# The high halves of a mixer's weight tiles: from GpSimd to ScalarE

## The reference

```python
h = rmsnorm(x, norm_pre_mix) * (1 + scale_m) + shift_m      # scale, shift, gate: silu(c) @ w_ada + b_ada
proj = h @ w_in                                             # the widest product of the block
# attention: 12 heads of 128 in three dilated groups, rotary, softmax, sum over groups
y_attn  = attention(proj[...]) @ w_attn_out
# 16 DeltaNet heads: short convolution, silu, l2norm, gated delta rule in chunks, rmsnorm, silu gate
y_delta = gated_delta_rule(proj[...]) @ w_delta_out
y = (sigmoid(gates_a) * y_attn + sigmoid(gates_d) * y_delta) @ w_mix_out
x = x + gate_m * rmsnorm(y, norm_post_mix)
# then a PEER feed-forward block: queries, top-16 of 128 x 128 experts, gelu, weighted sum of expert rows
```

## Time and profile before

| | |
|---|---|
| Median of 3 executions | 5580.42 us (5576.69 to 5580.77) |
| Profiled execution, its own time | 5584.36 us |
| Its span, first to last instruction | 5582.6 us |
| Mean granted TensorE clock | 0.970 |
| TensorE busy | 5186.8 us (93%) |
| VectorE busy | 2819.2 us (51%) |
| ScalarE busy | 1427.8 us (26%) |
| GpSimd busy | 2954.6 us (53%) |

### The profile page before, as it was taken

How to read it: one execution, slowest core, us unless ns; L and a number is a source line. 1 busy time by engine, 2 the same in 40 slices (tenths; PEclk the granted TensorE clock), 3 DMA queues, 4 the chain that set the end, 5 groups by cost and what they waited for, 6 DMA issues and landing times.

```text
span 5582.6 us, 67218 instructions
## 1 busy us (share of the span) xinstructions
PE 5186.8 (93%) x25699; PEld 4417.7 (79%) x25699; DVE 2819.2 (51%) x4370; ACT 1427.8 (26%) x2021; POOL 2954.6 (53%) x1124
## 2 busy tenths in 40 slices
PE   3877899998999899999989999999999999999997
PEld 1666778777777777877858888888888799999997
DVE  7777730455555545224367756664000056666764
ACT  2100010133232332100032233333222233333332
POOL 1454457644444444577734443334444478888883
PEclk6988899999999999999999999999999999999999
DMA  7444422311111111232323334344333479988994
GB/s 303 177 166 177 175 97 90 121 61 60 56 60 60 61 56 62 73 120 105 112 105 110 111 126 148 133 149 151 132 121 119 138 247 317 316 314 308 317 316 146
DMA packets 245042, 839.93 MB, mean 150 GB/s; under 512 B 24080, under 2 KB 89744, under 8 KB 200624
## 3 DMA queue, kind: packets, MB, share of 16 engines
q1 hardware_dynamic: 127632, 562.09, 29.0%
q10 hardware_dynamic: 94752, 141.98, 7.5%
q0 software_dynamic: 22528, 134.30, 6.3%
HBM read 766.91 MB, written 71.37 MB: 150 GB/s over the span
## 4 chain that ended last, share of the span: by engine, by line
PE 71%; DVE 13%; issue 7%; DMA 4%; ACT 2%; POOL 1%; ACTq 1%; SPq 0%; DVEq 0%
PE bank L835 9%; PE bank L837 9%; PE bank L839 9%; PE bank L518 7%; PE bank L520 6%; PE bank L522 6%; PE bank L932 5%; PE bank L934 5%; PE bank L933 5%; DVE hacc L1555 4%; DMA half<-ada_late 3%; PE bank L898 2%; PE wide L743 1%; PE wide L732 1%; DMA raw<-stream 1%
## 5 line engine op out<-in xcount | busy, mean ns | idle before, releaser
L460 POOL TENSOR_TENSOR lo<-raw,hi 128x1024 fp32r<-128x1024 f32 x528 | 1279.0, 2424 | 1147.1 <-ACT hi L1244 1143.5
L444 POOL TENSOR_TENSOR hi<-raw,ones 128x2048 fp32r<-128x2048 f32 x168 | 610.6, 3635 | 1354.8 <-PE bank L522 1084.7
L518 PE MATMUL bank<-xh,hi 128*128 128x512 f32 x2624 | 1111.9, 424 | 39.1 <-DVE xl L1485 11.5
L520 PE MATMUL bank<-xl,hi 128*128 128x512 f32 x2624 | 1040.0, 396 | 0.0
L522 PE MATMUL bank<-xh,lo 128*128 128x512 f32 x2624 | 1039.5, 396 | 0.0
L835 PE MATMUL bank<-xh,hi 128*128 128x512 f32 x2176 | 858.9, 395 | 8.8 <-DVE xl L1485 8.8
L1244 ACT ACTIVATE hi<-raw 128x1024 fp32r<-128x1024 f32 x528 | 546.7, 1056 | 1215.4 <-PE bank L839 1043.4
L837 PE MATMUL bank<-xl,hi 128*128 128x512 f32 x2176 | 848.0, 390 | 0.0
L839 PE MATMUL bank<-xh,lo 128*128 128x512 f32 x2176 | 847.7, 390 | 0.0
L447 POOL TENSOR_TENSOR lo<-raw,hi 128x2048 fp32r<-128x2048 f32 x168 | 819.2, 4876 | 13.2
L932 PE MATMUL bank<-CH,hi 128*128 128x384 f32 x2048 | 694.5, 339 | 16.1 <-DVE R L1944 8.3
(11 more groups left out here) (275 smaller groups left out, 5985.7 us busy)
## 6 DMA issues: line engine op xcount, KB each, us to landing
raw<-stream SPq DMA_DIRECT2D x528, 512.0 KB, 3.9
raw<-stream SPq DMA_DIRECT2D x184, 1024.0 KB, 4.8
half<-ada_late SPq DMA_DIRECT2D x128, 512.0 KB, 3.9
act_d<-etile ACTq DMA_DIRECT2D x128, 256.0 KB, 2.0
G_d<-stage ACTq DMA_DIRECT2D x12, 2048.0 KB, 7.5
Gt<-G_d ACTq DMA_DIRECT2D x32, 768.0 KB, 15.3
cf<-act_d ACTq DMA_DIRECT2D x31, 768.0 KB, 18.1
arow<-stream SPq DMA_DIRECT2D x16, 1024.0 KB, 7.3
```

What stands on the lines that cost most here:

```text
L444: nc.gpsimd.tensor_tensor(hi[slot][:, :], raw[s][:, :], ones[:, 0:1].to_broadcast([P, D]), ALU.mult).then_inc(hi_done, 1)
L460: nc.gpsimd.tensor_tensor(lo_h[slot], raw_h[h % 4], hi_h[slot].bitcast(F32), ALU.subtract).then_inc(f_lo[h % 4], 1)
L518: nc.tensor.matmul(out, hi[slot][:, w], at_k(xh, k), start=(k == 0), stop=False, skip_group_check=True)
L520: nc.tensor.matmul(out, hi[slot][:, w], at_k(xl, k), start=False, stop=False, skip_group_check=True)
```

## The change

`split` goes. GpSimd waits only for `hi_done` and subtracts. ScalarE gets `high(s, turn)`, a copy of the whole tile that waits for the raw tile and for the slot's unit, at written-out places in its own order: the two first tiles in steps 6 and 10 of the making of `h`; behind the copy of each attention unit and each gate unit; in a loop of their own for `w_attn_out` and `w_delta_out`; in the DeltaNet ahead of the unit's tanh, behind `ahead_of_unit`; for `w_mix_out` ahead of the square of each row block.

```diff
         @block.gpsimd
         def _(pool):
-            def split(s, slot, landed, free, count):
-
-                pool.wait_ge(raw_full[s], landed)
-                if free is not None:
-                    pool.wait_ge(unit_done[slot], free + ONE)
-                nc.gpsimd.tensor_tensor(hi[slot][:, :], raw[s][:, :], ones[:, 0:1].to_broadcast([P, D]), ALU.mult
-                                        ).then_inc(hi_done, 1)
-                pool.wait_ge(hi_done, count)
-                nc.gpsimd.tensor_tensor(lo[slot][:, :], raw[s][:, :], hi[slot][:, :].bitcast(F32),
-                                        ALU.subtract).then_inc(raw_used[s], 1)
-
-            pool.wait_ge(s_const, 1)
-            for s in (2, 3):
-                pool.wait_ge(arow_used[s], ADA_USES + ONE)
             with pool.Fori(0, MIX_USES) as i:
                 for s in range(2):
-                    split(s, s, (ADA_USES + 1 + i) * 16, i, i * 2 + s + 1)
+                    pool.wait_ge(hi_done, i * 2 + s + 1)
+                    nc.gpsimd.tensor_tensor(lo[s][:, :], raw[s][:, :], hi[s][:, :].bitcast(F32), ALU.subtract
+                                            ).then_inc(raw_used[s], 1)
...
+            def high(s, turn):
+
+                act.wait_ge(raw_full[s], (turn + (ADA_USES + 1)) * 16)
+                act.wait_ge(unit_done[s], turn + ONE)
+                nc.scalar.activation(hi[s][:, :], raw[s][:, :], ACT.Copy).then_inc(hi_done, 1)
+
...
                     shifted(k - 1, R1, R1, part(SHIFT_M), s_hr)
+                if k in (6, 10):
+                    s = (k - 6) // 4
+                    act.wait_ge(arow_used[2 + s], ADA_USES + ONE)
+                    high(s, 0)
...
                     nc.scalar.activation(dst[:, :], bank[u % 2][:, :], ACT.Copy).then_inc(bank_free[u % 2], 1)
+                    high(u % 2, u // 2 + 1)
...
+                high(s, i + (B_GA // 2 + 1))
...
+            for w in range(U_WAO):
+                high(w % 2, (B_WAO + w) // 2 + 1)
             act.wait_ge(s_waoc, 3 * U_WAO)
...
                     if not first:
                         ahead_of_unit(h - 1, j)
+                    high(j % 2, h * 2 + (B_DN // 2 + j // 2 + 1))
                     if j < 3:
                         act.wait_ge(d_e, h * 3 + j)
...
+                high(s, i + (B_GD // 2 + 1))
...
+            for u in range(U_WDO):
+                high(u % 2, (B_WDO + u) // 2 + 1)
             act.wait_ge(unit_done[1], B_MIX // 2 + ONE)
...
             for k in range(KT):
+                if k < U_MIX - 2:
+                    high(k % 2, (B_MIX + k) // 2 + 1)
                 act.wait_ge(bank_free[k % 2], B_MIX // 2 + k // 2 + 1)
```

## The result

| | before | after |
|---|---|---|
| median | 5580.6 us (5576.69 to 5588.56, 4 runs) | 5481.31 us (5479.76 to 5484.19, 4 runs) |
| ratio | | 0.9821 [0.9804, 0.9838] |
| profiled execution, and its span | 5584.36, 5582.6 us | 5480.44, 5478.6 us |

The kernel is 99 us faster (104 in the profiled executions).

What follows compares the result with a forecast made beforehand. VectorE, held up by GpSimd and with the DMA loop of `half`, was taken to pace attention. Terms: -51 attention, +5 start, +4.4 DeltaNet, -3 product starts, +1 last attention-out tile = -43.6 us; forecast 5537 us, range 5500 to 5580.

Steps and rivals of the forecast that it cites:

- the attention term: Attention stretch: VectorE is held up less by GpSimd and units get shorter, 1.5 us a unit, -51 us.
- 75 us is the most if all returns: Attention: upper bound of the gain, 36 high halves with about 2.1 us of VectorE waiting in each.
- the start: First tiles: ScalarE's high half comes late, TensorE starts 7 us later, first product near 134; taken as +5 us.
- The replay: Attention: one cycle of two units, 38.1 us from softmax to softmax, worked through; 3.6 us shorter.
- The price that the prediction feared: Attention: a VectorE operation in flight makes GpSimd's low half wait; at worst 28 us off the 51, leaving 23.
- The DeltaNet: DeltaNet heads: low halves end later in three of four units, earlier in the fourth; +0.3 us a head, +4.4 us.
- The step that I replayed first: DeltaNet, behind the unit ending at 1571.6: `q` becomes free, but `bt` and TensorE's next step end 0.54 us later.
- Gate units: Gate stretch: the split takes 7.3 us after a unit's end, covered by TensorE's next unit of 10.5; unchanged.
- delta-out and mix-out products: Their starts wait for the same lock, which ends 1 to 1.5 us earlier each: -3 us with both.
- The low half's end is all that counts: Rival, chance 0.12: VectorE's work is caught by the low half anyway; attention gives only 20 us, 5567 us.
- ScalarE's order makes the DeltaNet slower: Rival, chance 0.14: high halves ahead of each convolution's tanh delay TensorE, 5.8 us a head; 38 us slower, 5618.
- The DeltaNet gains too: Rival, chance 0.10: the shorter lock removes a third of the DeltaNet's 105 us idle, 35 us more; 5497 us.

Runs made afterwards that it cites:

- relock: Kernel after, with GpSimd's old multiplication put back ahead of the low halves of tiles 2 to 37, ScalarE still making the high halves: 5581.73 us.
- nolock: Kernel after, with two GpSimd fills, which read nothing, and two one-column operations ahead of the low halves of tiles 2 to 37: 5499.36 us.
- experiment 4: Kernel after, with ScalarE making the first two high halves ahead of h instead of in its steps 6 and 10: 5477.13 us.
- light_hacc: Kernel before, with hacc, all but the first of each sum, on 128 of its 1024 columns: 5508.39 us against 5580.38.
- attention_only: Kernel after, but GpSimd splits as before for all but the first 38 tiles: 5488.21 us against 5582.03 for the kernel before.
- before_in_two: Kernel before, with both of GpSimd's halves in two pieces and nothing on ScalarE: 5532.14 us, ratio 0.9907 to before.
- rest_only: Kernel after, but GpSimd splits the first 38 tiles as before: 5573.22 us, ratio 0.9981 to before.
- low_two: Kernel after, with each low half as two GpSimd operations instead of one: 5403.07 us, ratio 0.9682 to before.
- early_low_four: Kernel after, with each low half in four pieces and ScalarE's first two high halves ahead of h: 5337.01 us, ratio 0.9552 to before.

## Why the prediction was wrong, point by point

**The step that failed is the attention term.** It was sized at -51 us, 1.5 a unit, with "75 us is the most if all returns". From TensorE's first product to the end of tile 36's low half the kernel took 777.8 - 127.2 = 650.6 us and now takes 669.7 - 132.7 = 536.9: -114, 3.2 for each of 35 units. With the start, -46 was forecast and -108 measured. The mechanism was the right one (relock and nolock), the size was off by a factor of two. Two places in the working can be pointed to, and a third, the clock, may have its part.

*The bound counted too little.* The 75 us were the waiting inside the high halves alone. But 33 of VectorE's 111 us come from the rotation of `qk`, which the low half had caught (4.43 us instead of 0.67 at 392.75) and which now runs ahead of it. When one hold goes, what stands behind it moves, and may escape the next one. The bound is then the whole waiting in the stretch, not the share of the instruction removed: the earlier trace rows had it, 154 us for `hacc` alone.

*The replay kept the old phase.* It moved each end by its own saving, but left TensorE's unit where it stood against VectorE's softmax. The timelines of VectorE and of GpSimd in the kernel after, one cycle of two units, for the earlier trace rows:

```profile
352.23 0.41 DVE L1537 SCALAR_TENSOR_TENSOR prob<-wide,acst 128x256 f32<-128x256 f32 x1
...
356.53 0.75 DVE L1550 TENSOR_SCALAR prob<-prob,mcol 128x1024 f32<-128x1024 f32 x1
...
357.80 0.67 DVE L1527 TENSOR_TENSOR qk<-qk,acst 32x512 f32<-32x512 f32 x1
...
359.11 2.67 DVE L1563 SCALAR_TENSOR_TENSOR hacc<-half,cond,hacc 128x1024 f32<-128x1024 f32 x2
363.71 4.98 DVE L1563 SCALAR_TENSOR_TENSOR hacc<-half,cond,hacc 128x1024 f32<-128x1024 f32 x2 [1.94 <-DMA half<-ada_late]
...
382.16 0.41 DVE L1537 SCALAR_TENSOR_TENSOR prob<-wide,acst 128x256 f32<-128x256 f32 x1
```

```profile
345.19 4.57 POOL L442 TENSOR_TENSOR lo<-raw,hi 128x2048 fp32r<-128x2048 f32 x1 [7.86 <-ACT hi L977]
360.86 5.36 POOL L442 TENSOR_TENSOR lo<-raw,hi 128x2048 fp32r<-128x2048 f32 x1 [11.09 <-ACT hi L977]
```

The cycle is 382.16 - 352.23 = 29.9 us; 38.1 was the old one and 34.6 the replay's. The low half begins 8.6 us behind the softmax's first step, in the replay 6.4. The rotation is done ahead of it in both. But in these 2.2 us two `hacc` get in as well (2.67 us for both, so free), which the replay had end with the low half. So the shorter cycle for VectorE changed what the low half meets. The price that the prediction feared shows in the same place: the low half takes 5.36 us because the second of them is still running. This account is read from two timelines; no run moves the phase alone.

**The granted clock.** In the attention stretch it is 0.98 after and 0.88 before, means over the levels of 2.4 and 1.2 GHz, and a multiplication takes 463.52/2097 = 0.221 us instead of 486.62/2046 = 0.238. What TensorE did before was to wait: the 64 us at L621 are gone. relock brings 0.89 back with the old waits, nolock has 0.96. Of the 114 us from the first product to tile 36, TensorE's busy time makes up 37 (547.3 to 510.5 us) and its idle time 77 (103.4 to 26.5). So the clock moves with the hold. How much of the gain is its own can't be told apart, since no run changes it alone: in a stretch that VectorE paces, TensorE's shorter busy time need not shorten anything. The prediction held TensorE's own 487 us fixed.

**The start**, +5 for the start with a first product near 134: it is at 132.75, +5.6. The step was right as a time, but as the start of the paced stretch it was worth less (experiment 4).

**The DeltaNet**, +4.4: +6.4 from tile 60 to 120. The nearness of the two numbers is luck. The step that I replayed first went as worked out. VectorE's timeline in the kernel after, the step of the earlier trace rows; GpSimd's, for the earlier trace rows; TensorE's wait:

```profile
1472.92 0.69 DVE L1702 SCALAR_TENSOR_TENSOR dn_q<-dn_q,dn_rs 128x512 f32<-128x512 f32 x1 [3.43 <-ACT dn_rs L1096]
...
1476.54 3.84 DVE L1624 TENSOR_TENSOR dn_bt<-dn_LT,cst 128x512 f32<-128x512 f32 x1
...
1520.12 0.75 DVE L1690 SCALAR_TENSOR_TENSOR R<-dn_T,dn_w,dn_z 128x512 f32 x1
```

```profile
1475.25 4.58 POOL L442 TENSOR_TENSOR lo<-raw,hi 128x2048 fp32r<-128x2048 f32 x1 [16.51 <-ACT hi L977]
```

```profile
1481.18 1.04 PE L720 MATMUL wide<-dn_X,dn_bt 128*128 128x128 f32 x7 [2.77 <-DVE dn_XT L1631]
```

`q` is free (0.69 us), `bt` starts earlier and gains nothing by it: 1476.54 + 3.84 = 1480.38, 0.55 behind the low half's 1479.83, as forecast. `R` is free too. But TensorE's waits of the whole stretch, tile 60 to 120, before and after, add up the other way:

```profile
PE wide L732 <- DVE dn_XT L1623: 38.8, 15, 2.6
PE bank L753 <- DVE dn_s L1631: 27.5, 15, 1.8
PE bank L725 <- DVE dn_bt L1654: 19.2, 15, 1.6
...
PE wide L758 <- DVE dn_r L1669: 6.3, 11, 0.9
```

```profile
PE wide L720 <- DVE dn_XT L1631: 41.4, 15, 2.8
PE wide L746 <- DVE dn_r L1677: 32.1, 14, 2.3
...
PE bank L713 <- DVE dn_bt L1662: 5.0, 15, 0.5
PE bank L741 <- DVE dn_s L1639: 4.6, 15, 0.3
```

The wait at the step above grows by 0.17 us a head, where 0.54 was forecast. That for `dn_r` grows by 1.7 a head, those for `dn_s` and for L1654 shrink by 1.5 and 0.9. TensorE's idle time falls by 7 us, where the forecast had it rise by 4.4. The profiled executions of other kernels, over the same 60 tiles, show that this holds and why the time hides it:

| kernel | high halves in the DeltaNet | us | TensorE busy | idle | granted clock |
|---|---|---|---|---|---|
| before | GpSimd | 1168.9 | 1065.1 | 103.8 | 0.99 |
| light_hacc | GpSimd | 1182.8 | 1076.7 | 106.1 | 0.97 |
| attention_only | GpSimd | 1194.5 | 1088.2 | 106.3 | 0.96 |
| before_in_two | GpSimd, both halves cut | 1197.4 | 1091.7 | 105.8 | 0.96 |
| after | ScalarE | 1175.3 | 1078.9 | 96.4 | 0.97 |
| rest_only | ScalarE | 1177.9 | 1081.6 | 96.3 | 0.97 |
| low_two | ScalarE, low half cut in 2 | 1122.0 | 1056.4 | 65.6 | 0.99 |
| early_low_four | ScalarE, low half cut in 4 | 1075.2 | 1046.9 | 28.3 | 1.00 |

The first three have the same code there and differ by 26 us, 23 of them TensorE's busy time, which goes with the granted clock. The profiled execution of the kernel before was a short one in this stretch. The change takes 7 to 10 us of TensorE's idle time away, which fits the 9 us of rest_only. So this term had the wrong sign; why the clock differs between executions of the same code stays open.

**The small terms.** Gate units unchanged: TensorE has 257.57 of 260 us. The tiles in which the delta-out and mix-out products start (137 to 138 and 153 to 154) are 1.3 and 1.6 us shorter, -2.9 for -3. A term was left out: the first units of the DeltaNet, tile 56 to 60, take 51.1 us instead of 46.9, and TensorE waits there once for a square of ScalarE's, 2.6 us. The low half is 4.66 us, 4.94 in the attention stretch (163.17/33) against 5.30 before: the 28 us by which it might have been slowed did not come.

**The rivals.** *The low half's end is all that counts*: no. nolock ends it 1.8 us later, keeps 82% of the gain and was timed once. *ScalarE's order makes the DeltaNet slower*: no; rest_only is not slower. *The DeltaNet gains too*: not the 35 us of the rival, some 7 to 10 of idle time. But it named the lever: once the low half is cut, TensorE's idle time there goes from 96 us to 66 (low_two) and 28 (early_low_four).

**The range** reached to 5500 only for the third rival. With 154 us as the bound of the attention term its low end would have lain below the result.

## What to carry to other kernels

Where VectorE works with two SBUF inputs and sets the pace, count GpSimd's instructions that read SBUF by the time that they hold, not by their own place in the schedule. Move them to an engine that holds nothing (11 `hacc` operations of the kernel after begin beside ScalarE's copy alone, and all take 1.26 to 1.29 us), and cut what stays into short pieces. Here 3.8 us of multiplication ahead of each of 36 low halves cost 100 us, and cutting the low halves in four saved another 140. When you replay a cycle, let the other engines' phase move with it. Bound the gain by all the waiting that the hold causes, and look at what the clock may add. And before you read a difference of a few us between two executions as the change's, split it into TensorE's busy and idle time.

## What the hardware showed that I had not expected

- VectorE gets in between two GpSimd instructions that follow each other at once. That is why 5.55 us in four pieces hold it up less than 4.66 us in one.
- A hold costs roughly in proportion: 0.66 us of the kernel's time for one held at 2.02 us, 0.60 to 0.73 at 3.83 us, each timed once.
- A fill on GpSimd (1.81 us for 128x2047) did not hold VectorE up: 39 `hacc` operations that began beside one took 1.27 to 1.29 us. Beside the multiplication 21 of 22 took 2.07 to 4.44.
- A VectorE operation on one tile and a column of one value a partition was held up as well: L1542 took 2.69 us at 389.54, beside GpSimd's high half, and takes 0.75 at 356.53 in the kernel after.
- At an eighth of its columns 68 of 120 `hacc` operations took under 0.5 us and the other 52 up to 4.68: a small operation is held up as long as a large one.
- TensorE's granted clock in the attention stretch rose from 0.88 to 0.98 as its waits went.
- The same code of the DeltaNet took 1168.9, 1182.8 and 1194.5 us in three kernels, with TensorE idle for 103.8 to 106.3 us and a granted clock of 0.99, 0.97 and 0.96.
